# Two attention heads' score products in one TensorE step, one head in rows 0 to 63 and the other in rows 64 to 127

## What is computed

```
# mo, di (first block):        sc = q @ k.T * 64**-0.5 + slope * distance (masked);  softmax;  @ v
# a2 (second block, 8 heads x 2 halves):
sc = einsum('bqhmd,bkhmd->bhmqk', qblk, k) * 64**-0.5
p = softmax(where(allowed, sc, -inf)); w = p[:, :, 0] - lam_full * p[:, :, 1];  w @ v
# c (second block, 16 heads):
z = einsum('bqhd,bkhd->bhqk', qb, k) * 64**-0.5
log_stay = where(strict, log_sigmoid(-z), 0); after = reverse_cumsum(log_stay) - log_stay
a = where(strict, exp(log_sigmoid(z) + after), 0);  a @ v
```

## Time and profile before

| | |
|---|---|
| median of three runs | 2971.26 us (2970.50 to 2974.64) |
| the profiled execution's own time | 2972.2 us |
| its span | 2970.4 us |
| TensorE matmul (PE) busy | 2905.7 us, 98% of the span |
| TensorE weight load (PEld) busy | 2568.9 us, 86% |
| VectorE (DVE) busy | 1877.6 us, 63% |
| ScalarE (ACT) busy | 1481.7 us, 50% |
| DMA | 504.12 MB, 170 GB/s on average, queue busy 47.6% |

### The profile page before, as it was taken

How to read it: one execution, slowest core, us unless ns; L and a number is a source line. 1 busy time by engine, 2 the same in 40 slices (tenths; PEclk the granted TensorE clock), 3 DMA queues, 4 the chain that set the end, 5 groups by cost and what they waited for, 6 DMA issues and landing times.

```text
span 2970.4 us, 45312 instructions
## 1 busy us (share of the span) xinstructions
PE 2905.7 (98%) x18276; PEld 2568.9 (86%) x18276; DVE 1877.6 (63%) x2790; ACT 1481.7 (50%) x2300; POOL 179.0 (6%) x158
## 2 busy tenths in 40 slices
PE   8999999999999999999999999999999999999998
PEld 8979879989989779989878878889799788878897
DVE  5655666656555566655468777665554687786654
ACT  5445555444445545444445567444344465565442
POOL 0000010000000010000014100110100131000100
PEclk9999999999999999999999999999999999999999
DMA  6544345555543345545544343555455453444553
GB/s 236 182 154 147 136 143 184 189 176 189 199 150 123 140 156 198 199 170 199 185 168 170 128 156 135 198 185 185 172 197 187 171 180 128 149 142 167 202 186 126
DMA packets 74493, 504.12 MB, mean 170 GB/s; under 512 B 8720, under 2 KB 10416, under 8 KB 18352
## 3 DMA queue, kind: packets, MB, share of 16 engines
q1 hardware_dynamic: 74288, 501.24, 47.6%
HBM read 500.12 MB, written 1.08 MB: 169 GB/s over the span
## 4 chain that ended last, share of the span: by engine, by line
PE 93%; DVE 4%; ACT 1%; issue 1%; DMA 0%; POOL 0%; SPq 0%; DVEq 0%; ACTq 0%
PE ps L1409 46%; PE ps L1427 38%; PE ps L1448 3%; PE ps L1528 2%; PE ps L1527 1%; DVE wlo L1852 1%; PE ps L1554 1%; PE ps L1553 1%; DVE x L1921 1%; PE ps L1552 1%; ACT whi L1596 0%; DVE x L1965 0%; DVE conv L2145 0%; DVE xT_lo L1875 0%; DMA raw<-in_w 0%
## 5 line engine op out<-in xcount | busy, mean ns | idle before, releaser
L1596 ACT ACTIVATE whi<-raw 128x1024 fp32r<-128x1024 f32 (+3 forms) x938 | 977.6, 1043 | 906.9 <-PE ps L1409 486.7
L1852 DVE TENSOR_TENSOR wlo<-raw,whi 128x1024 fp32r<-128x1024 f32 (+4 forms) x923 | 1107.5, 1213 | 314.8 <-ACT whi L1596 314.3
L1427 PE MATMUL ps<-xT_hi,whi 128*128 128x256 f32 x3296 | 928.9, 282 | 5.7 <-DVE conv L2145 3.0
L1427 PE MATMUL ps<-xT_lo,whi 128*128 128x256 f32 x3296 | 920.9, 279 | 0.0
L1427 PE MATMUL ps<-xT_hi,wlo 128*128 128x256 f32 x3296 | 920.4, 279 | 0.0
L1427 PEld LDWEIGHTS ps<-xT_hi,whi 128*128 128x128 f32 x3296 | 620.1, 188 | 17.9 <-issue 17.2
L1427 PEld LDWEIGHTS ps<-xT_lo,whi 128*128 128x128 f32 x3296 | 620.3, 188 | 0.6
L1427 PEld LDWEIGHTS ps<-xT_hi,wlo 128*128 128x128 f32 x3296 | 620.0, 188 | 0.0
L1409 PE MATMUL ps<-whi,xT_hi 128*128 128x512 f32 (+2 forms) x1152 | 466.7, 405 | 32.9 <-issue 16.2
L1409 PE MATMUL ps<-whi,xT_lo 128*128 128x512 f32 (+2 forms) x1152 | 452.2, 393 | 0.0
L1409 PE MATMUL ps<-wlo,xT_hi 128*128 128x512 f32 (+2 forms) x1152 | 452.1, 392 | 0.0
(11 more groups left out here) (313 smaller groups left out, 2638.3 us busy)
## 6 DMA issues: line engine op xcount, KB each, us to landing
raw<-in_w SPq DMA_DIRECT2D x437, 1024.0 KB, 4.8
raw<-in_w SPq DMA_DIRECT2D x20, 768.0 KB, 4.3
vr<-in_vrows SPq DMA_DIRECT2D x19, 512.0 KB, 5.7
sums<-scratch SPq DMA_DIRECT2D x8, 512.0 KB, 4.7
raw<-in_w SPq DMA_DIRECT2D x3, 832.0 KB, 4.4
raw<-in_w SPq DMA_DIRECT2D x2, 928.0 KB, 4.6
raw<-in_w SPq DMA_DIRECT2D x2, 576.0 KB, 3.7
x<-in_x SPq DMA_DIRECT2D x2, 512.0 KB, 5.3
```

The costliest lines, as they stand in the source:

```text
L1427: made = e.matmul(out, ws[:, o:o + 128], xs[:, kt, :], start=kt == 0 and n == 0 and c % 2 == 0, stop=kt == job.nk - 1 and n == 2, skip_gro ...
L1596: e.activation(out, raw, ACT.Copy).then_inc(*mark("hi", i))
L1852: e.tensor_tensor(out, raw, hi.bitcast(F32), sub).then_inc(*mark("lo", i))
```

## The change

For the heads that are 64 wide the scores of two heads become one TensorE step `qk`, issued in the turn of the even head: it waits for q and k and for both banks, then issues the first product of the even head and of the odd head, then the second product of both. Each head has its own bank. In the odd head's turn TensorE has no scores to issue; VectorE's and ScalarE's steps stay in the turns in which they were. mla heads use the same new step with one head in it.

```diff
+    def qk(self, heads, after):
+        banks = [self.aux.get() for _ in heads]
+        self.do("qk", heads, after, banks)
+        return [b for b, _ in banks]
-    def scores(self, key, qT, kT, after, scale, bias, bias_there, nm, den, sms, slope=1.0):
-        ps, free = self.aux.get()
+    def scores(self, key, ps, scale, bias, bias_there, nm, den, sms, slope=1.0):
         sm, sm_free = sms.get()
-        self.do("scores", key, qT, kT, after, ps, free, sm, sm_free, scale, slope, bias, bias_there, nm)
+        self.do("scores", key, ps, sm, sm_free, scale, slope, bias, bias_there, nm)
         self.aux.put(ps, ("scores", *key))
...
@@ heads (mo, di); heads_a and heads_c alike
-                    rr = slice(64 * (h % 2), 64 * (h % 2) + 64)
+                    if s % 2 == 0:
+                        banks[s], banks[s + 1] = self.qk([((kind, l, h + j), qk[rows[j], qb, :], qk[rows[j], kb, :])
+                                                          for j in (0, 1)], (qk_there[qb], qk_there[kb]))
...
@@ tensor_program
-    def qk_products(ps, qT, kT):
-        e.matmul(ps[:, 0:128], qT[:, 0:128], kT[:, 0:128], start=True, stop=True)
-        return e.matmul(ps[:, 128:384], qT[:, 128:256], kT[:, 0:256], start=True, stop=True)
-
-    def scores(key, qT, kT, after, ps, free, *_):
-        for f in (*free, *after):
+    def qk(heads, after, banks):
+        for f in after:
             pe.wait_ge(*at(*f))
-        qk_products(ps, qT, kT).then_inc(*mark("att", *key))
-
-    def stick_scores(l, h, qT, kT, after, ps, free, *_):
-        for f in (*free, *after):
-            pe.wait_ge(*at(*f))
-        qk_products(ps, qT, kT).then_inc(*mark("att", "s", l, h))
+        for _, free in banks:
+            for f in free:
+                pe.wait_ge(*at(*f))
+        for (_, qT, kT), (ps, _) in zip(heads, banks):
+            e.matmul(ps[:, 0:128], qT[:, 0:128], kT[:, 0:128], start=True, stop=True)
+        for (key, qT, kT), (ps, _) in zip(heads, banks):
+            e.matmul(ps[:, 128:384], qT[:, 128:256], kT[:, 0:256], start=True, stop=True
+                     ).then_inc(*mark("att", "s", *key))
```

More of the change, by code:

```diff
@@ L782, in heads @@
             items = [("mo", h) for h in range(6)] + [("di", h) for h in range(12)]
-            probs, turned = {}, {}
+            probs, turned, banks = {}, {}, {}
+            rows = [slice(0, 64), slice(64, 128)]
             for s in range(len(items) + 4):
@@ L796, in heads @@
                     table, slope = (3, SLOPES[12 + h]) if kind == "mo" else (h // 4, SLOPES[h])
-                    probs[s] = self.scores((kind, l, h), qk[rr, qb, :], qk[rr, kb, :], (qk_there[qb], qk_there[kb]),
-                                           0.125, m["dist"][:, table, :], ("dist",), nm, den, sms, slope)
+                    probs[s] = self.scores((kind, l, h), banks[s], 0.125, m["dist"][:, table, :], ("dist",), nm, den,
+                                           sms, slope)
                 if 0 <= s - 2 < len(items):
@@ L883, in mla_heads @@
                     b = turned[h]
-                    probs[h] = self.scores(("mla", l, h), b[:, 0:256], b[:, 256:512], (("copy_a", "mlaT", l, h),),
-                                           96.0 ** -0.5, m["causal"][:, :], ("causal",), self.stat(2), self.stat(2),
-                                           sms)
+                    ps, = self.qk([(("mla", l, h), b[:, 0:256], b[:, 256:512])], (("copy_a", "mlaT", l, h),))
+                    probs[h] = self.scores(("mla", l, h), ps, 96.0 ** -0.5, m["causal"][:, :], ("causal",),
+                                           self.stat(2), self.stat(2), sms)
                     ring.put(b, ("scores", "mla", l, h))
@@ L1130, in heads_a @@
         def heads_a():
-            probs, w, pT = {}, {}, {}
+            probs, w, pT, banks = {}, {}, {}, {}
             for s in range(16 + 5):
@@ L1154, in heads_a @@
                 if s < 16:
[L1155 to L1159, removed]
+                    h = s // 2
+                    if s % 2 == 0:
+                        banks[s], banks[s + 1] = self.qk(
+                            [(("a2", l, s + j), qka[64 * j:64 * j + 64, h, :], qka[64 * j:64 * j + 64, 8 + h, :])
+                             for j in (0, 1)],
+                            (("copy_a", "qka", l, h - h % 2), ("copy_a", "qka", l, 8 + h - h % 2)))
+                    probs[s] = self.scores(("a2", l, s), banks[s], 0.125, m["chunk"][:, :], ("chunk",),
+                                           self.stat(2), self.stat(2), sms)
                 yield
@@ L1190, in heads_c @@
             self.do("log_table")
-            z_of, w_of, pT = {}, {}, {}
+            z_of, w_of, pT, banks = {}, {}, {}, {}
             for s in range(16 + 5):
@@ L1207, in heads_c @@
                 if s < 16:
-                    rr = slice(64 * (s % 2), 64 * (s % 2) + 64)
                     b = s // 2
-                    ps, free = self.aux.get()
+                    if s % 2 == 0:
+                        banks[s], banks[s + 1] = self.qk(
+                            [(("c", l, s + j), qkc[64 * j:64 * j + 64, b, :], qkc[64 * j:64 * j + 64, 8 + b, :])
+                             for j in (0, 1)], (qkc_there(b), qkc_there(8 + b)))
                     z, z_free = sms.get()
                     w, w_free = prs.get()
-                    self.do("stick_scores", l, s, qkc[rr, b, :], qkc[rr, 8 + b, :], (qkc_there(b), qkc_there(8 + b)),
-                            ps, free, z, z_free, w, w_free)
-                    self.aux.put(ps, ("scores", "c", l, s))
+                    self.do("stick_scores", l, s, banks[s], z, z_free, w, w_free)
+                    self.aux.put(banks[s], ("scores", "c", l, s))
                     z_of[s], w_of[s] = z, w
@@ L1810, in log_table, with stick_scores @@
         e.preload_act_table_set(LN2)
-    def stick_scores(l, h, qT, kT, after, ps, free, z, z_free, w, w_free):
+    def stick_scores(l, h, ps, z, z_free, w, w_free):
         act.wait_ge(*at("scores", "c", l, h))
@@ L1966, in add_x, with scores @@
                                    ).then_inc(*mark("xnew", s, t, n))
-    def scores(key, qT, kT, after, ps, free, sm, sm_free, scale, slope, bias, bias_there, nm):
-        dve.wait_ge(*at("att", *key))
+    def scores(key, ps, sm, sm_free, scale, slope, bias, bias_there, nm):
+        dve.wait_ge(*at("att", "s", *key))
         dve.wait_ge(*at(*bias_there))
@@ L2233, in oa_out, with stick_scores @@
                         bc(r, 128), mul).then_inc(*mark("vec", "oa", l, h))
-    def stick_scores(l, h, qT, kT, after, ps, free, z, z_free, w, w_free):
-        dve.wait_ge(*at("att", "s", l, h))
+    def stick_scores(l, h, ps, z, z_free, w, w_free):
+        dve.wait_ge(*at("att", "s", "c", l, h))
         dve.wait_ge(*at("strict"))
```

4 lines of the change are left out of this document (2 added, 2 removed).

## The result

The change takes the median to **2937.07 us** (2934.93 to 2938.42, four runs) beside 2970.88 us for the kernel before on the same chip (2969.44 to 2974.64): ratio 0.9884, 95% interval 0.9866 to 0.9901, 33.8 us less. The forecast was 2946.8 us, its range 2939 to 2954 us. The side was right; the gain of 24.5 us was too small, and the measured time lies 2 us under the range.

A forecast was written before the change was run, and what follows sets the result against it. TensorE was taken to bound the kernel, its matmuls busy for 98% of the span. Fewer height changes, 19.0 us, plus side by side, 5.5 us, made 24.5 us off 2971.3 us: 2946.8 us, range 2939 to 2954 us.

The forecast's parts named there:

- TensorE is the bound, what it is spared comes off the end.: Where the heads run, time spared TensorE shortens the end, as long as VectorE and ScalarE keep up; 24.5 us in all.
- 50 changes to 64 rows and back less, 19.0 us.: Score steps: 100 steps with 64 rows become 50, each sparing 0.38 us lost at its two ends, 19.0 us.
- Side by side, 0.11 us per pair, 5.5 us.: Paired score products: only the joint between the two 256-column products overlaps, 0.11 us per pair, 5.5 us.
- the lower bound: Paired score products: the odd head's all vanish beside the even head's, 0.66 us per pair, 33 us.
- hidden whole: Rival at the paired score products: whole odd head hidden, 33 us, 2919.3 us; chance within the 0.09 for much overlap.
- much overlap: Rival at the paired products: 22 us if loads did not limit, 33 us if odd head hidden whole; chance 0.09.
- Changing halves empties the array too: Rival at a pair's three joints between halves: 0.19 us each, 9.5 us slower, 2980.8 us; chance 0.07.
- Banks cost nothing, 0.90 and 0.99 us of cover.: Score banks of a2 and c: needed one turn earlier, still free 0.90 and 0.99 us ahead, so no cost.
- The bank rival: In a2 and c, VectorE or banks take back 32 pairs' gains of 0.49 us, 15.7 us: 2962.5 us at worst; chance 0.05.

The follow-up runs named there:

- head-after-head run: The changed kernel with a pair's four products reordered, both of the even head, then both of the odd head: 2937.07 us, ratio 0.9885.
- The two reorderings: Changed kernel with exps behind oa_out in a2's odd turns and stick_scores ahead of stick in c's odd turns: 2920.72 us, ratio 0.9830.
- the experiment: The unpaired kernel before, with only the first block's mo and di heads contracting over rows 0 to 95: 2955.54 us, ratio 0.9951.

## Why the prediction was right or wrong, point by point

- *TensorE is the bound, what it is spared comes off the end.* Right in the first block (0.98 us per pair of 1.04), wrong in the second, where the 32 pairs brought 16.2 of 33.3 us because the chains of VectorE, ScalarE and GpSimd were nearer than the prediction took them to be. (A 9 in the page's row of the clock stands for 90% or more; the mean granted clock before was 0.995 of full speed, in the change 0.996, so the clock has no part in it.)
- *50 changes to 64 rows and back less, 19.0 us.* Right: 17.6 us with both heads in one half, and 0.39 us per step where all of it could be seen alone.
- *Side by side, 0.11 us per pair, 5.5 us.* This is the step that failed first. The prediction assumed that matmuls start in the order of the program and that all loads share one pace of 0.11 us. Both assumptions came from rows in which no two neighbouring products lay in different halves. Measured is the lower bound that the prediction had named and set aside: 0.66 us per pair, 33 us. The rival "hidden whole" had only a part of the 0.09 for much overlap.
- The Trainium skill, "TensorE: Matmul & The Clock Gate", section "Part 3: Packing small matmuls", had the time of a packed pair right: the two halves' first matmuls start 7 ns apart in the records of a di pair, where the page gives about 4 ns. The same section says that matmuls are never reordered; the head-after-head run shows the opposite between the halves, and the measurement decides.
- *Changing halves empties the array too* (the slower rival). Out: in a pair nothing is lost between the halves. This agrees with what the Trainium skill says in "TensorEngine Tiling (Array Packing)", section "Key Properties", that changing the tiling mode drains TensorE and changing only the tile does not.
- *Banks cost nothing, 0.90 and 0.99 us of cover.* Wrong, the second step that failed. The cover was worked out for one turn, but TensorE comes sooner in every pair, and the chain that frees the bank has its own length and does not follow. In the changed kernel the first a2 pair that needs a bank of `oa_out` still has 0.98 us of cover (L2243 ends at 1653.18, the pair starts at 1654.16), near the 0.90 worked out; the next has 0.42 us (1661.41, 1661.83), and from then on TensorE waits, 0.80, 0.48 and 1.07 us. In c the cover is down to 0.06 us, and the hand-over between VectorE and ScalarE sets the pace. The bank rival had the place (a2's and c's banks, VectorE 88% busy), but its chance was 0.05, and that its 15.7 us are near the 18 us lost is chance: it took back gains of 0.49 us per pair in full, where some 0.5 of 1.04 us per pair were lost. The two reorderings returned 17 of the 18 us.
- The two errors had opposite signs: 33 instead of 5.5 us is 27.5 us too little, and some 18 us were lost that were put at nothing. That the total misses by only 9.7 us is luck.

What stays open: no run puts both heads of a pair into one bank, or tries more than two orders of issue, and it is not known what part of the last 3 of the 18 us is more than scatter.

## What to carry to other kernels

Two products of 64 rows in different halves of TensorE, each with its own bank, cost as much as one here (0.86 us for a pair of heads, 0.85 us for one), and of the two orders of issue that were tried, both between the same two full-height products, neither was better. A step over 64 rows between full-height ones costs 0.38 us in itself, so gather such steps, also where they cannot overlap (17.6 us in the run with both heads in one half). When an engine at 98% is relieved, work out the round time of the others per unit of work (18.19 us for four c heads, where TensorE needed only 17.06), not the slack at one place: here a reordering that was worth nothing before the change was worth 17 us after it.

## What was not expected of the hardware

- The two halves of the array were fed out of order with each other: with both products of the even head first in the program, the odd head's first still started 13 to 14 ns after the even head's first, in all 50 pairs. Loads and matmuls of both interleave so fully that eight instructions take the time of four (0.49 and 0.60 us, for float32 products of 128 and 256 columns).
- A step over 96 rows between full-height products costs only its streaming, 0.66 us; one over 64 rows costs 0.38 us more (0.39 us in the experiment), in the two changes of height around it.
